# Two blocks on one core: where the units of differential attention stand beside the input panels, and how the mLSTM's decay weights are made

## The reference

```python
# mLSTM, 4 heads of 128, here done for all 512 tokens at once
logD = where(causal, b[t] - b[s] + ig[s], -inf)
m_t  = max(b + m, max_s logD);   Dw = exp(logD - m_t)
sqk  = (q @ k.T) * Dw
num  = sqk @ v;   den = sum(sqk)
h    = num / max(|den|, exp(-m_t))          # then rmsnorm per head, times sigmoid(mo)

# differential attention, 4 heads, two score maps each, in blocks of 128 queries
s   = where(kpos <= qpos, (q @ k.T) * scale, NEG)      # p = 0, 1
a   = softmax(s)
att = a[0] - lam * a[1]
o   = att @ v                               # then rmsnorm per head
```

## Time and profile before

| | |
|---|---|
| median of 3 runs | 2567.14 us (2561.35 to 2574.85) |
| the profiled execution | 2568.06 us |
| its span, first to last instruction | 2566.3 us |
| TensorE busy over the span | 2186.5 us (85%) |
| VectorE busy | 1402.3 us (55%) |
| ScalarE busy | 640.4 us (25%) |
| POOL busy | 884.1 us (34%) |
| mean granted TensorE clock | 0.917 of full speed |

### The profile page before, as it was taken

The page is one execution under the profiler, slowest core; times in us unless marked ns, Lnnn a source line. Parts: engine busy times, 40 slices in busy tenths (PEclk is TensorE's granted clock), DMA queues, the critical chain, the costliest instruction groups (busy, mean ns, idle before and its releaser), DMA issues.

```text
span 2566.3 us, 31438 instructions
## 1 busy us (share of the span) xinstructions
PE 2186.5 (85%) x12528; PEld 1625.9 (63%) x12528; DVE 1402.3 (55%) x2843; ACT 640.4 (25%) x1073; POOL 884.1 (34%) x822
## 2 busy tenths in 40 slices
PE   7987689999999997789799958789789888877775
PEld 6885488998998884687688835457678444411111
DVE  3237547677546465657789878669976133300000
ACT  3123333223245233232011114341111233300000
POOL 0023000000000000001356556546567666666664
PEclk8997899999999997799899978799899888899899
DMA  4200024444321210023699989879999999899997
GB/s 168 83 33 1 1 99 173 189 175 184 126 99 66 99 55 29 17 83 114 230 388 395 401 304 330 320 255 361 354 415 418 417 342 339 317 384 371 365 376 290
DMA packets 146483, 587.94 MB, mean 229 GB/s; under 512 B 16272, under 2 KB 16401, under 8 KB 133665
## 3 DMA queue, kind: packets, MB, share of 16 engines
q0 software_dynamic: 110592, 402.70, 41.5%
q1 hardware_dynamic: 34560, 176.70, 18.3%
q10 hardware_dynamic: 1184, 6.53, 0.6%
HBM read 582.19 MB, written 3.67 MB: 228 GB/s over the span
## 4 chain that ended last, share of the span: by engine, by line
PE 49%; DVE 25%; issue 8%; POOL 7%; DMA 4%; another core or an unknown queue 4%; ACT 3%; DVEq 0%; ACTq 0%; SPq 0%; POOLq 0%
PE ps L539 11%; PE ps L541 10%; PE ps L540 10%; DVE cols L1888 9%; PE ps L1063 6%; POOL big L2439 5%; PE ps L1013 3%; DMA big<-utab,cols 1%; DMA big<-vtab,big 1%; POOL hres L2439 1%; DVE big L1706 1%; DVE big L1712 1%; DVE cols L1708 1%; ACT Ir L2287 1%
## 5 line engine op out<-in xcount | busy, mean ns | idle before, releaser
L1000 PE MATMUL ps<-rowb,raw 128*128 128x256 f32 x2048 | 466.2, 388 | 36.3 <-DMA raw<-ucols 21.7
L1000 PEld LDWEIGHTS ps<-rowb,raw 128*128 128x128 f32 x2048 | 393.7, 195 | 105.8 <-issue 19.4
L1063 PE MATMUL ps<-big,cols 128*32 128x512 f32 x1380 | 374.2, 688 | 68.5 <-issue 46.0
L2439 POOL DMA_INDIRECT big<-vtab,big x345 | 339.8, 985 | 196.6 <-issue 86.5
L2352 POOL TENSOR_TENSOR small<-small,cols 128x1 f32<-128x1 f32 (+3 forms) x33 | 27.8, 841 | 909.1 <-DVE small L1449 385.8
L1063 PEld LDWEIGHTS ps<-big,cols 128*32 128x32 f32 x1380 | 72.7, 119 | 248.6 <-issue 158.8
L2439 POOL DMA_INDIRECT big<-utab,cols x144 | 173.6, 1205 | 125.2 <-DVE big L1888 50.5
L1888 DVE CUSTOM_DVE_ANT_0 cols<-big 128x1024 f32<-128x1024 f32 x144 | 176.6, 1226 | 46.3 <-DMA big<-utab,cols 27.7
L1013 PE MATMUL ps<-Aj,Ir 128*128 128x64 f32 x1024 | 157.8, 300 | 19.3 <-issue 15.7
L2276 ACT ACTIVATE Aj<-ps 128x512 f32<-128x512 f32 x64 | 67.9, 1067 | 409.0 <-PE ps L1000 349.4
L539 PE MATMUL ps<-xhb,whb 128*128 128x512 f32 (+1 forms) x432 | 166.3, 385 | 3.5 <-issue 2.1
(11 more groups left out here) (386 smaller groups left out, 4641.2 us busy)
## 6 DMA issues: line engine op xcount, KB each, us to landing
raw<-ucols SPq DMA_DIRECT2D x128, 512.0 KB
raw<-ff SPq DMA_DIRECT2D x32, 1024.0 KB, 4.9
raw<-w SPq DMA_DIRECT2D x24, 1024.0 KB, 4.9
raw<-ada SPq DMA_DIRECT2D x24, 1024.0 KB, 4.8
raw<-wo SPq DMA_DIRECT2D x8, 1024.0 KB, 4.9
raw<-wq SPq DMA_DIRECT2D x8, 1024.0 KB, 4.9
big<-vtab,big POOLq DMA_INDIRECT x345
out<-hres SPq DMA_DIRECT2D x7, 512.0 KB, 8.3
```

The source lines that it names most:

```text
L1000: ins = e.matmul(PS[b][:, c:c + 256], lhsT=un[j % NU][:, k, :], rhs=h2T[k // 4][:, k % 4, :], start=(k == 0), stop=(k == 7))
L1063: ins = e.matmul(PS[hf][32 * j:32 * j + 32, :], lhsT=win[:, c0:c0 + 32], rhs=gs[i][:, hf * 512:(hf + 1) * 512], start=(m == 0), stop=(m == ...
L2439: e.indirect_dma_start(gs[i], None, utab if st == "U" else vtab, bass.IndirectOffsetOnAxis(ap=idx, axis=0)).then_inc(sems[f"l_g{i}"], 16)
```

## The change

All 16 units, with t = 0 to 3, stand beside six panels (10, 11, 12, 13, 8, 9): both chains take eight units each, with maps of 512 columns that lie in the buffer of the mLSTM's later output. Panel 10 is no longer alone. The mLSTM's steps follow; only the last turns of the units stand beside its first steps, and the units' turn now comes first there. The sigmoid stands one panel turn later. The mLSTM's mask becomes an addition of a large negative number (`caus`), made in the gate bank itself for the 128 columns of the step's diagonal block; ScalarE takes the exponent straight from the bank, with the gate term as its bias; the subtract-and-clip step and the multiplication by the mask go. Scores use four banks (1, 3, 4, 5), so a score matmul waits for the product four steps back. The head norms of the attention are due at turns 7, 13, 19 and 25, and POOL takes all of them ahead of the mLSTM's. The squares go to a buffer that the gates used before. The diff below is cut; it goes from the shared set-up to the programs of TensorE, VectorE and ScalarE.

```diff
-        EARLY = [[(t, h) for t in range(3) for h in (i, i + 2)] for i in range(2)]
...
+        UNITS = [[(t, h) for t in range(NT) for h in (i, i + 2)] for i in range(2)]
+        maps = [[hoMf[:, 1024 * i + 512 * p:1024 * i + 512 * p + 512] for p in range(2)] for i in range(2)]
+        sqb = {"m": rowb[:, 0:512], "d": rowb[:, 512:1024]}
...
-        DUE = {"d": [(0, 7), (1, 13), (2, 21), (3, 33)], "m": [(h, 4 * h + 8) for h in range(4)]}
+        DUE = {"d": [(t, 6 * t + 7) for t in range(NT)], "m": [(h, 4 * h + 8) for h in range(4)]}
...
-            return (1, 5 if s > 3 else 7)[s % 2]
+            return (1, 3, 4, 5)[s % 4]
...
-            def diff(units, b0, b1):
+            def diff(x):
+                b0, b1, (P0, P1) = 3 + 2 * x, 4 + 2 * x, maps[x]
...
                     P.wait_ge(*at["df_c", (t, h)])
+                    P.wait_ge(*at["ev_a", "dv", h // 2, t])
...
-            pv = panel("w2", 10)
-            projR(sb_, pv, 0, CW, ("dv", 0), "ev_a", rows4)
-            panel_done("w2", 10)
...
-            for t in range(NT):
-                P.wait_ge(*at["ev_a", "dv", 0, t])
-            units = lagged(*((i, diff(UNITS[i], 3 + 2 * i, 4 + 2 * i)) for i in range(2)))
-            for i, name, ev in ((11, ("dv", 1), "ev_a"), (12, ("mo", 0), "ev_a"), (13, ("mo", 1), "ev_a"),
+            P.wait_ge(*at["ev_v", "dk", 3, 0])
+            units = lagged(*((i, diff(i)) for i in range(2)))
+            for i, name, ev in ((10, ("dv", 0), "ev_a"), (11, ("dv", 1), "ev_a"), (12, ("mo", 0), "ev_a"), (13, ("mo", 1), "ev_a"),
                                 (8, ("mv", 0), "ev_v"), (9, ("mv", 1), "ev_v")):
...
             def gates_of(h):
                 if h == 1:
-                    P.wait_ge(*at["df_h", (2, 3)])
+                    P.wait_ge(*at["df_h", (3, 3)])
                 if h > 1:
-                    P.wait_ge(*at["ml_d", h - 2, NT - 1])
+                    P.wait_ge(*at["ml_e", h - 2, NT - 1])
...
             def ml_scores(s):
                 h, j = divmod(s, NT)
-                if s > 1:
-                    P.wait_ge(*at["ml_w", divmod(s - 2, NT)])
+                if 0 < s < 4:
+                    P.wait_ge(*at["df_h", (3, 3 if s == 3 else 2)])
+                if s > 3:
+                    P.wait_ge(*at["ml_w", (h - 1, j)])
...
-            beside(mlstm(), units)
+            beside(units, mlstm())
...
                 for s in range(4 * NT + 4):
                     h, j = divmod(s, NT)
+                    if s < 4 * NT:
+                        b = PS[(0, 6)[h % 2]][:, j * 128:(j + 1) * 128]
+                        V.wait_ge(*at["ml_m", h])
+                        if j:
+                            V.wait_ge(*at["ml_e", h, j - 1])
+                        if s == 0:
+                            V.wait_ge(*V.last)
+                        e.tensor_tensor(b, b, col("caus"), ALU.add).then_inc(*V.mark("ml_d", h, j))
                     if 0 < s <= 4 * NT:
...
-                        e.tensor_tensor(Dt[:, 0:128], Dt[:, 0:128], col("caus"), ALU.mult).then_inc(*V.mark())
...
-                        e.tensor_scalar(Dts[s % 2][:, 0:TX - j * 128], PS[(0, 6)[h % 2]][:, j * 128:TX],
-                                        ac[:, 4 * j + h:4 * j + h + 1], 0.0, ALU.add, ALU.min).then_inc(*V.mark("ml_d", h, j))
...
                         e.scalar_tensor_tensor(out=Wts[hw % 2][:, jw, jw * 128:TX], in0=PS[score_bank(s - 1)][:, 0:w],
-                                               scalar=128.0 ** -0.5, in1=Dt[:, 0:w], op0=ALU.mult, op1=ALU.mult
+                                               scalar=128.0 ** -0.5, in1=Dts[(s - 1) % 2][:, 0:w], op0=ALU.mult, op1=ALU.mult
...
-            beside(mlstm(), units, head_norm("m"))
+            beside(units, mlstm(), head_norm("m"))
...
             def mlstm():
+                A.wait_ge(*at["used", unit["w2", 9]])
                 for h in range(4):
                     for j in range(NT):
-                        Dt = Dts[j % 2][:, 0:TX - j * 128]
+                        s = 4 * h + j
                         A.wait_ge(*at["ml_d", h, j])
-                        e.activation(Dt, Dt, ACT.Exp).then_inc(*A.mark("ml_e", h, j))
+                        if s > 1:
+                            A.wait_ge(*at["ml_w", divmod(s - 2, NT)])
+                        e.activation(Dts[s % 2][:, 0:TX - j * 128], PS[(0, 6)[h % 2]][:, j * 128:TX], ACT.Exp,
+                                     bias=ac[:, 4 * j + h:4 * j + h + 1]).then_inc(*A.mark("ml_e", h, j))
                         yield
...
-                    if (i, t) == (9, 1):
+                    if (i, t) == (9, 2):
                         e.activation(mo, mo, ACT.Sigmoid).then_inc(*A.mark("ev_a", "mo", "gate"))
...
-    c["caus"] = (j <= i).astype(np.float32)
+    c["caus"] = np.where(j <= i, 0.0, BIGNEG)
```

More of the change, by code:

```diff
@@ L834, in tensor_program @@
                     panel_done("w2", i + g)
-            def diff(units, b0, b1):
+            def diff(x):
+                b0, b1, (P0, P1) = 3 + 2 * x, 4 + 2 * x, maps[x]
                 prev = None
-                for t, h, P0, P1 in units:
+                for t, h in UNITS[x]:
                     n = (t + 1) * 128
-                    if (t, h) == (3, 0):
-                        yield
-                        yield
                     for p, b in ((0, b0), (1, b1)):
@@ L1546, in head_norm, with diff @@
                     e.tensor_tensor(o3, o3, gate, ALU.mult).then_inc(*V.mark("hn_o", i, k))
-            def diff(units, x, b0, b1):
+            def diff(x):
+                b0, b1, (P0, P1) = 3 + 2 * x, 4 + 2 * x, maps[x]
                 so = sm[:, 276 + 12 * x:288 + 12 * x]
-                for t, h, P0, P1 in units:
+                for t, h in UNITS[x]:
                     n = (t + 1) * 128
-                    if (t, h) == (3, 0):
-                        yield
-                        yield
                     for p, b in ((0, b0), (1, b1)):
@@ L1614, in vector_program @@
                         evict((name, 2 * g + a, 0), dst[:, 2 * g + a, :], 128, TX)
-            panel("w2", 10)
-            units = lagged(*((i, diff(UNITS[i], i, 3 + 2 * i, 4 + 2 * i)) for i in range(2)), (0, head_norm("d")))
-            for i in (11, 12, 13, 8, 9):
+            units = lagged(*((i, diff(i)) for i in range(2)), (0, head_norm("d")))
+            for i in (10, 11, 12, 13, 8, 9):
                 for t in range(NT):
@@ L2181, in head_norm @@
                         A.wait_ge(*at["hn_s", i, past])
-                    if (i, k) == ("d", 2):
-                        A.wait_ge(*at["used", unit["w2", 9]])
-                    e.activation(square_of(i, k).rearrange("p (n c) -> p n c", c=128), normed[i][k][0], ACT.Square
+                    e.activation(sqb[i].rearrange("p (n c) -> p n c", c=128), normed[i][k][0], ACT.Square
                                  ).then_inc(*A.mark("hn_a", i, k))
@@ L2229, in scalar_program @@
                 panel("w2", i)
-            panel("w2", 10)
-            evict_rows(("dv", 0), dv, 0)
-            units = lagged(*((i, diff(UNITS[i], i, 3 + 2 * i, 4 + 2 * i)) for i in range(2)), (0, head_norm("d")))
-            for i in (11, 12, 13, 8, 9):
+            units = lagged(*((i, diff(i)) for i in range(2)), (0, head_norm("d")))
+            for i in (10, 11, 12, 13, 8, 9):
                 panel("w2", i)
@@ L2417, in head_norm @@
                 power(r4[:, 4 * k:4 * k + 4], s4[:, 4 * k:4 * k + 4], 128, 4).then_inc(*G.mark("hn_r", i, k))
-            for i, k in (("d", 0), ("d", 1), ("d", 2), ("m", 0), ("m", 1), ("d", 3), ("m", 2), ("m", 3)):
-                head_norm(i, k)
+            for i in ("d", "m"):
+                for k in range(4):
+                    head_norm(i, k)
             fence(8)
```

33 lines of the change are left out of this document (4 added, 29 removed).

## The result

The changed kernel takes 2536.27 us (median of four runs, 2533.68 to 2539.87) beside 2564.24 us of the kernel before on the same chip (four runs, 2560.54 to 2574.85): a ratio of 0.9885, 95% interval 0.9852 to 0.9919, so 28 us or 1.15% less. The forecast was 2545 us, with 2530 to 2561 as its range. The profiled execution took 2539.9 us with a span of 2538.0 (before: 2568.1 and 2566.3).

A forecast was written before the change was run, and what follows sets the result against it. The prediction took TensorE to bound the panels, and engines waiting in turns, none full, to bound the 81.40 us mLSTM stretch. It summed 2568.1 + 16.8 + 1.2 - 41.4 = 2544.7 us, say 2545, range 2530 to 2561.

The forecast's parts named there:

- Part 1: Panel 10 and the t = 3 units moved beside the panels: +16.8 us, bounds +11.8 and +22.
- The stall of round 22: Beside the panels, TensorE waits for a VectorE copy behind the next weight panel's remainder: 2.7 us of stall.
- the last copy of dk: At the start of the 24 panel rounds, a new wait of TensorE for this copy: some 0.7 us.
- Part 2: Handover from the last panel tile to the first gate rows, longer by +1.2 us (0 to +2.7).
- The sigmoid's chain: At the handover: masks, maxima, exponents, table load and sigmoid, ending 6.7 us after the scores of round 22.
- Part 3: The mLSTM alone, first gate rows to last product: 40 us in place of 81.4, so -41.4 us.
- the middle of 31 and 49: mLSTM stretch taken as 40 us, between 31 us at 2.4 GHz and 49 us at 1.2 GHz.
- the working for 2.4 GHz: mLSTM stretch bound by VectorE: 14.3 us lead, two heads at 7.0, 2.5 for the last two products, 31 us.
- Low clock throughout: Rival: TensorE stays at the low clock through the mLSTM; stretch 49 us, total 2554 us; chance 0.14.
- taking turns still: Rival: score, exponent and product in the mLSTM can't overlap; stretch 80.3 us, total 2585 us; chance 0.05.
- beside the t = 3 units the clock was lost: Rival: a stall in round 18 or 19 drops TensorE to 1.2 GHz; +17 us, total 2562; chance 0.07.
- the change doesn't do what it says: Rival: last units still stand between mLSTM steps, or VectorE's load beside the last panels exceeds TensorE's; 2567 us; chance 0.04.

The follow-up runs named there:

- e6: Changed kernel with two weight-panel remainders on VectorE moved, one a round earlier, one to the mLSTM's first step: 2533.95 us against 2537.45.
- e7: Changed kernel without the last multiplication of each head norm on VectorE, executed once: stretch from first gate rows to last product 34.2 us against 33.9.
- e8: Changed kernel with every head's gate-row matmul issued twice on TensorE, executed once: stretch from first gate rows to last product 35.0 us against 33.9.
- e1: Kernel before with only the units moved beside the panels, old exponents and two score banks: 2440.80 us, 0.9894 of the kernel before.
- e5: Changed kernel run again unaltered, as the measure for e6, e7 and e8 on the same chip: 2537.45 us, 0.9904 of the kernel before.
- e9: Changed kernel run once more unaltered on a further chip, as the measure for e10: 2535.50 us, 0.9896 of the kernel before.
- e2: Changed kernel with two banks of scores in place of four: 2431.55 us, 0.9856 of the kernel before.
- e10: Changed kernel with the output gates' sigmoid earlier on ScalarE and the gate-column copy ahead of VectorE's long multiplication: 2528.93 us against 2535.50 for e9.
- the first four experiments: Kernels holding one or two of units moved, mask in the bank, four score banks, on another chip: ratios to the kernel before 0.9856 to 0.9971.
- e4: Kernel before with only the mask in the bank and ScalarE's exponents out of it, two banks, units not moved: 2453.74 us, 0.9971.

## Why the prediction was right, step by step

The sum was 2568.1 + 16.8 + 1.2 - 41.4. Measured in the profile: +14.1, +1.6, -47.5, which makes 2536.3; the profiled execution took 3.6 us more, the ones after the next projection's start. So the sum was 8.4 us too high, 6.1 of them in part 3. That 2536.3 is also the median of the four runs is luck.

- **Part 1, +16.8 expected, +14.1 measured.** The stall of round 22 came where it was put, behind the remainder, but with 1.65 us instead of 2.7 (the sign put down was over 2 us); round 10's stayed (2.2). The last tile was costed at the low clock throughout (+2.3); it won the clock back on its way and took 3.98 us (990.51 to 994.49), 1.2 over a tile at full clock. These two terms are 2.2 of the 2.7 us. The wait for the last copy of dk cost 1.1 instead of 0.7. The 24 tiles with their rounds took 112.4 us from the first tile on, where about 115 were put down. The bounds, +11.8 and +22, held.
- **Part 2, +1.2 expected, +1.6 measured.** First gate rows 5.3 to 5.4 us after the tile, where 5.0 were worked out. The sigmoid's chain was right to the tenth (it ends 6.6 us after the scores of round 22, where 6.7 were worked out), and it, not the last unit's weighting, is what the multiplication then waits for, by 0.49 us. The step was read too narrowly: I priced the sigmoid's chain as a time of the handover alone and didn't see that behind the wait it makes TensorE take the mLSTM's first head can lose its clock (2.9 us in e6, 3.1 in e7).
- **Part 3, -41.4 expected, -47.5 measured.** The mechanism was right: turns between engines gone (21.1 to 1.6 us of waits), VectorE as the pace (e7, e8). The mis-sized term is the choice of 40 us as the middle of 31 and 49. The upper end was not in play: the clock in the stretch is 0.96 until VectorE has done its last product, and the working for 2.4 GHz holds within a microsecond to there. These are the first masks of the third and the fourth head, and that last product:

```profile
1014.01 0.29 DVE L1652 TENSOR_TENSOR ps<-ps,cols 128x128 f32<-128x128 f32 x1
...
1021.40 0.29 DVE L1652 TENSOR_TENSOR ps<-ps,cols 128x128 f32<-128x128 f32 x1
...
1028.80 0.28 DVE L1660 SCALAR_TENSOR_TENSOR over<-ps,over 128x128 f32<-128x128 f32 x1
```

  The third head's first mask was put at 14.3 us and came after 14.1; the two heads behind it were put at 7.0 each and took 7.39 and 7.68. Only the last two products cost 4.67 us at half the clock, behind a wait of 4.47, where 2.5 were put down. So 33.9, not 30.8, and not 40.
- **What misled me** was the earlier trace rows and the mean of 0.66, read as what this work does to the clock. In that stretch TensorE waited in every turn, and the earlier trace rows begins right behind a wait of 3.76 us. This is the first line of those 7.8 us:

```profile
1039.42 0.80 PE L907 MATMUL ps<-big 128*128 128x128 f32 x2 [3.76 <-DVE over L1676]
```

  But in those 7.8 us it was busy throughout and the clock didn't rise; no run here shows why. The Trainium skill (TensorE: Matmul & The Clock Gate, Part 1) calls the lower level the default that activity lifts; the stretch alone, with few waits in it, agrees (0.96), and so does the drain behind the one long wait (0.50); the busy 7.8 us of the earlier trace rows at 0.50 don't show the lifting.
- **The mask in PSUM.** The Trainium skill (VectorE: DVE Perf Modes, section on the TRN2 errata) has the larger fixed cost on the PSUM side; measured are 294 ns against 286, so by the trace the difference is small, as before (0.1 us over the 16 masks). The part pays off because it takes the subtract-and-clip steps away: 8 us of VectorE, and the stretch is 5.8 to 8.4 us shorter with it.
- **The rivals.** Low clock throughout (49 us) and taking turns still (80 us) are excluded by the stretch; beside the t = 3 units the clock was lost in round 22 only. The last one, that the change doesn't do what it says, did not come true for the units. One part came to little: four banks instead of two let VectorE end 2.8 us earlier in the profiles with the mask in the bank, and moved nothing clear of the spread in the whole stretch.

What stays open: why the low clock is met at the handover in one profile of the changed kernel and not in two others, why it didn't rise over the earlier trace rows, and where the 3.6 us after the next projection's start come from, beyond that such differences appear between profiles of one kernel.

## What to carry to other kernels

Two pieces of work that alternate on every queue can cost more than their sum: here 81.3 us together, against 33.9 for the one alone (40.4 with the old exponents, e1) and 14.1 for the other beside the panels. Each waited at the other's turn, and TensorE's clock was lower (0.66, later 0.90). Put them one after the other, the short one beside work that fills TensorE. Before a stage is costed at either clock, ask what its waits will be after the change, not what they were before. And when a stage gets faster, look at what it now waits for at its end: here the 6.0 us won beside the panels shrank to 3.2 with a longer wait for an old chain on ScalarE and a first head at 0.60 of the clock behind it; with that chain moved into an idle stretch, 8.8 us came out.

## What the runs showed of the hardware

- The price of a wait is not its length alone. A wait of 2.89 us (e6) was followed by 7.36 us for a head that takes 4.49 otherwise; a wait of 1.82 us in the same place (e5) was followed by no loss in that head. In e8 the same wait of 1.82 us, with twice the gate rows behind it, was followed by a head at 0.75. In a third profile of the changed kernel (e9) 0.82 and 1.10 us with 1.6 us of work between them were followed by a clock of 0.72.
- At the end of the mLSTM the same 20 matmuls took 2.50 us behind a wait of 2.23 us (e2, clock 1.00), 3.82 behind 2.83 (e1, 0.62), and 4.67 behind 4.47 (the changed kernel, 0.50); but 4.14 behind the same 4.47 in e10 (0.59).
- An exponent of ScalarE out of PSUM with a bias per row took 525 ns on the mean of four widths, where the one in SBUF without a bias took 466; which of the two differences costs the 59 ns was not told apart. For VectorE the bank made 8 ns.
- The chip of the first four experiments ran the same program 100 us faster (2462.62 against 2564.24 us). Up to the mLSTM the profiles agree (first gate rows at 983.75 in e4, at 984.21 in the kernel before); the gap lies behind it (from the next projection to the end 1381.5 us in e4, 1490.5 in the kernel before), most of all where gathers fill the DMA engines: from 2000 to 2430 they moved 419 GB/s in e4 and 360 in the kernel before. What makes the chips differ is not shown.
